# Moving hosted work to later slots in the expert stream of a fused two-layer transformer kernel

## What is computed

```python
for layer in range(DEPTH):
    y, y_x = token_mixer(modulate(x, sh1, sc1), modulate(ctx, xsh1, xsc1), w_in[layer], ...)
    x = layer_norm(alpha * x + g1 * y, ln1_g[layer], ln1_b[layer])
    f = peer(modulate(x, sh2, sc2), w_pq[layer], sub_keys[layer], u_tab[layer], v_tab[layer])
    x = layer_norm(alpha * x + g2 * f, ln2_g[layer], ln2_b[layer])
    # the context tokens go the same way, in layer 0 only

# peer, for a block of 128 tokens
q = (xb @ w_pq).reshape(128, 8, 2, 128)
s = einsum('thpd,hpnd->thpn', q, sub_keys)      # then top 16 of each half, top 16 of the 256 sums
u, v = u_tab[expert], v_tab[expert]             # 128 rows of each per token
a = gelu(einsum('td,thkd->thk', xb, u)) * softmax(top)
return einsum('thk,thkd->td', a, v)
```

## Time and profile before

| | us |
|---|---|
| median of three runs | 4543.57 |
| lowest, highest | 4536.91, 4545.58 |
| the profiled execution | 4533.96 |
| its span, first to last instruction | 4531.9 |

### The profile page before, as it was taken

The page is one execution under the profiler, slowest core; times in us unless marked ns, Lnnn a source line. Parts: engine busy times, 40 slices in busy tenths (PEclk is TensorE's granted clock), DMA queues, the critical chain, the costliest instruction groups (busy, mean ns, idle before and its releaser), DMA issues.

```text
span 4531.9 us, 47089 instructions
## 1 busy us (share of the span) xinstructions
PE 3090.0 (68%) x16196; PEld 1565.7 (35%) x16196; DVE 2892.1 (64%) x7342; ACT 823.3 (18%) x1929; POOL 2763.2 (61%) x2623
## 2 busy tenths in 40 slices
PE   7977787977678977645743778768698855443333
PEld 4443454444354343322310433445443422210000
DVE  4865677467676577556766663386756776766762
ACT  1321213122123131101110120221312310100100
POOL 1125666457667576657677665036666677777775
PEclk8989898998788998777865889989899976766556
DMA  8989999999999999999999999479999999999998
GB/s 326 331 296 403 398 408 383 367 360 406 404 406 393 409 388 396 407 408 404 393 397 366 397 392 408 170 260 410 395 390 401 371 404 408 403 382 394 399 405 332
DMA packets 494093, 1718.66 MB, mean 379 GB/s; under 512 B 54177, under 2 KB 74913, under 8 KB 493473
## 3 DMA queue, kind: packets, MB, share of 16 engines
q0 software_dynamic: 375552, 1367.51, 77.3%
q1 hardware_dynamic: 100640, 335.04, 19.2%
q10 hardware_dynamic: 17664, 13.11, 0.9%
HBM read 1700.25 MB, written 15.20 MB: 379 GB/s over the span
## 4 chain that ended last, share of the span: by engine, by line
PE 27%; POOL 26%; DMA 24%; issue 11%; DVE 9%; ACT 2%; SPq 0%; POOLq 0%; DVEq 0%; ACTq 0%
PE ps L983 26%; DMA vr<-in_v_tab,idxT 20%; POOL vr L956 14%; POOL ur L943 13%; DVE ur L2164 2%; PE ps L986 1%; DMA ur<-in_u_tab,idx 1%; DMA wring<-in_w_gb 1%; DMA wring<-in_w_mod 1%; DVE mx L2025 1%; DMA wring<-in_w_pq 1%; ACT arena L1490 0%; DVE rows L1836 0%; DVE vr L1836 0%; DVE mx L2023 0%
## 5 line engine op out<-in xcount | busy, mean ns | idle before, releaser
L2164 DVE CUSTOM_DVE_ANT_0 ur<-ur,hn 128x1024 f32<-128x1024 f32 x1280 | 1562.4, 1221 | 868.1 <-DMA ur<-in_u_tab,idx 864.2
L956 POOL DMA_INDIRECT vr<-in_v_tab,idxT x1256 | 1359.6, 1083 | 821.7 <-PE ps L983 485.2
L943 POOL DMA_INDIRECT ur<-in_u_tab,idx x1280 | 1351.9, 1056 | 753.0 <-issue 354.9
L983 PE MATMUL ps<-vr,spread 128*32 128x512 f32 x5024 | 889.0, 836 | 997.7 <-DMA vr<-in_v_tab,idxT 991.1
L983 PE MATMUL ps<-wring,arena 128*128 128x512 f32 (+1 forms) x2256 | 1025.4, 605 | 53.7 <-ACT arena L1490 15.2
L983 PEld LDWEIGHTS ps<-vr,spread 128*32 128x32 f32 x5024 | 180.7, 135 | 1490.7 <-issue 1488.6
L983 PEld LDWEIGHTS ps<-wring,arena 128*128 128x128 f32 x2256 | 422.3, 194 | 595.5 <-issue 529.1
L983 PE MATMUL ps<-hT,wring 128*128 128x128 f32 (+1 forms) x2048 | 315.9, 313 | 9.2 <-DMA wring<-in_w_pq 6.0
L983 PEld LDWEIGHTS ps<-hT,wring 128*128 128x128 f32 x2048 | 287.2, 199 | 76.3 <-issue 49.4
L986 PE MATMUL ps<-ident,arena 128*128 128x128 f32 x888 | 151.2, 306 | 119.6 <-ACT arena L1618 57.8
L983 PE MATMUL ps<-arena,wring 128*128 128x258 f32 (+1 forms) x960 | 223.5, 392 | 2.7 <-ACT arena L1577 2.2
(11 more groups left out here) (220 smaller groups left out, 2902.1 us busy)
## 6 DMA issues: line engine op xcount, KB each, us to landing
wring<-in_w_gb SPq DMA_DIRECT2D x224, 512.0 KB
wring<-in_w_pq SPq DMA_DIRECT2D x128, 512.0 KB
wring<-in_w_qkv SPq DMA_DIRECT2D x68, 512.0 KB
wring<-in_w_out SPq DMA_DIRECT2D x64, 512.0 KB
wring<-in_w_conv SPq DMA_DIRECT2D x60, 512.0 KB
wring<-in_w_mod SPq DMA_DIRECT2D x48, 512.0 KB
vr<-in_w_modt POOLq DMA_DIRECT2D x48, 512.0 KB, 7.8
ur<-in_u_tab,idx POOLq DMA_INDIRECT x1280
```

The costliest lines, as they stand in the source:

```text
L943: nc.gpsimd.indirect_dma_start(u, None, u_rows, bass.IndirectOffsetOnAxis(ap=idx[:, at:at + 1], axis=0)).then_inc(landed, 16)
L956: nc.gpsimd.indirect_dma_start(v, None, v_rows, bass.IndirectOffsetOnAxis(ap=idxT[:, pair % 3, i:i + 1], axis=0)).then_inc(landed, 16)
L983: return nc.tensor.matmul(o, lhsT, rhs, start=first, stop=last, skip_group_check=True)
L2164: v.tensor_tensor_reduce(u, u, hn[:], 1.0, 0.0, ALU.mult, ALU.add, dots[:, j % 2, k:k + 1]).then_inc(s["dots_done"], 1)
```

## The change

In tile 0 the loads of tile 1 stay at slot 0, and its near attention, first merge and ending stand at slots 12 to 64 instead of 0 to 62; the keys behind them at 64 to 74 instead of 62 to 74. In tile 6 the near keys stand at slot 11 instead of 0, the ending of tile 7 at 12 to 32 instead of 1 to 26, the reload at 32 instead of 26, and the remaining queries and the convolution at 42 to 69 instead of 33 to 68. No instruction and no transfer is added or removed.

```diff
@@ -292,8 +292,9 @@
         if n == 0:
-            put(near_part(1, team=1) + merge_first(1) + ending(1), 0, 62)
-            put(keys_job(1), 62, 74)
+            put([loads_of(1, team=1)], 0, 1)
+            put(near_part(1)[1:] + merge_first(1) + ending(1), 12, 64)
+            put(keys_job(1), 64, 74)
             put([[("turn", 1)], [("row", 0)], [("row", 1)], [("row", 2)]], 74, 78)
@@ -322,10 +323,10 @@
         elif n == 6:
-            put([[("nk", 0)]], 0, 1)
-            put(ending(7), 1, 26)
-            put(queries_job(4)[0:1], 26, 27)
-            put(queries_job(4)[1:] + conv_job(4), 33, 68)
+            put([[("nk", 0)]], 11, 12)
+            put(ending(7), 12, 32)
+            put(queries_job(4)[0:1], 32, 33)
+            put(queries_job(4)[1:] + conv_job(4), 42, 69)
             put([[("turn", 7)], [("row", 4)], [("row", 5)], [("row", 6)]], 74, 78)
```

## The result

The changed kernel takes **4573.4 us** (median, 4562.4 to 4590.4), beside 4543.1 us (4532.2 to 4549.7) for the kernel before on the same chip: ratio 1.0069, interval 1.0056 to 1.0083. It is slower, as forecast, but by 30 us instead of 12, and outside the range. The profiled execution has a span of 4584.2 us, 52.3 more than that of before.

What follows compares the result with a forecast made beforehand. The prediction took DMA, with a 410 GB/s ceiling, as the bound: unused DMA time adds 7.8 us (tile 6 to slot 32), 1 (its later slots) and 3.5 (tile 0), +12.3, giving 4556 us; own range 4547 to 4571.

Steps and rivals of the forecast that it cites:

- Bare slots: Slots 0 to 11 of tiles 0 and 6: 1.7 us each, set by DVE, 20.4 us with 2.4 unused.
- Attention: Tile 6's hosted attention: a chain of 38.8 us however few slots stand in it, 26.4 unused; tile 0's 26 us.
- Rival 1: Hosted chains in tiles 6 and 0 shrink with the slots in them: -5.4 us, 4538, not slower; chance 0.22.
- Merge of tile 6: Last merge with layer norm at slots 21.7 to 32: 38.4 us, 12.3 unused.
- Restart: Tile 6 after the ending: the reload waits for the ending's last write, now at slot 32; 2.6 us unused, as before.
- slot 40 is the next w_pq use, so nobody waits: Tile 6: w_pq chunks queued on SP behind the reload at slot 32 make no engine wait; no cost.
- rival 2: PE takes over from DMA in tile 6's slots 42 to 69 and tile 0's 41 to 64: 4566; chance 0.10.
- Tile 0: To slot 32, unused time rises from 12.9 to 16.4 us: +3.5, ends 0 and +6; later slots may leave 0 to 3 more.
- a longer wait costs nothing as long as transfers are queued: Tile 0 from slot 23: DVE's longer waits for merge chunks are free; far attention and end may leave 0 to 3 us.
- Nothing after slot 78 of either tile moves: Tiles 0 and 6 behind slot 78: stretches stay untouched, and any delay is simply carried to the end.
- rival 3: PE's lower clock level (1.2 GHz) holds for all of tile 6's attention: +5 us, 4561; chance 0.05.
- The sum: Whole kernel: 7.8 + 1 + 3.5 = +12.3 us, 4556 on the median, own range +3 to +27 us.

Runs made afterwards that it cites:

- e5: Kernel before with tile 6 hosting the ending of tile 7 at slots 1 to 16 instead of 1 to 26; ratio 1.0022.
- e10: Kernel before with only tile 6 changed: ending at slots 10 to 24, reload at 32, queries and convolution at 42 to 69; ratio 1.0033.
- e4: Kernel before with only tile 6's queries and convolution moved to slots 42 to 69, ending and reload as before; 4541.1 us, ratio 0.9993.
- e13: Tile 6 of the change alone, with the reload at slot 42 behind two w_pq chunks, queries at 43 to 69; 4550.5 us, ratio 1.0020.
- e11: Kernel before with only tile 0 changed: near attention stays at slots 0 to 13, merge and ending at 23 to 64, keys 64 to 74; ratio 0.9989.
- e8: Kernel before with only tile 0 changed: near attention, merge and ending at slots 12 to 70, keys at 70 to 74; ratio 1.0032.
- e1: Kernel before with only the change's tile 0 part (near attention, merge and ending at slots 12 to 64); 4551.1 us, ratio 1.0020.
- e18: The whole change with tile 6's reload at slot 42 behind two w_pq chunks, queries at 43 to 69; ratio 1.0023.
- e16: The kernel before, unchanged, run again for a trace on another chip; 4531.4 us.
- e12: Kernel before with tile 6's ending at slots 34 to 62, reload at 62, queries 63 to 86, near attention 90 to 127; ratio 1.0085.
- e9: Kernel before with tile 6's ending kept at slots 1 to 26, reload listed at 36, queries and convolution at 42 to 69; ratio 1.0002.
- e2: Kernel before with only the change's tile 6 part (ending at slots 12 to 32, reload 32, queries 42 to 69); 4558.6 us, ratio 1.0043.

## Why the prediction was right and wrong

**Bare slots: right.** Slots 0 to 12 of tile 6 took 20.0 us (forecast 20.4) with DVE busy 19.88 and 2.5 us unused (2.4). In tile 0 they took 19.0, with 3.1 unused (2.4).

**Attention: right.** From the first scores at 2995.73 to the merge it took 39.9 us (38.8) at 144 GB/s, unused 26.5 (26.4). In tile 0 the stretch from slot 12 to 24 took 26.9 (26), unused 10.7 (11.9). Rival 1 is refuted by this and by e5.

**Merge of tile 6: the term was mis-sized.** Forecast 38.4 us and 12.3 unused, measured 42.1 and 16.4. I had taken PE's part over from before, 25.8 us. But in before the query products of slots 24 and 25 stood behind it (at 3033.60), and the move brought the merge over those slots: 28.8 us with two products of 1.95 in it. e10 shows the same merge without them, 25.0. The tail was as before. Worth 4.1 us.

**Restart: the step "slot 40 is the next w_pq use, so nobody waits" failed.** The restart itself left 2.8 us (2.6). But the eight bare slots between the reload and slot 40 last only 16 us. Two w_pq chunks stood behind the reload on SP, and SP took 10.3 us to issue them while the first v gathers filled the engines. PE waits in order, so the v sums, the query products and POOL's v gathers wait with it. Slots 42 to 69 then carried what had been held up. I forecast 1 us there with ends 0 and 8; 4.6 us stand unused at slots 42 to 64. e4 shows that the dense queries by themselves cost nothing that can be told, and e13 that the order on SP is worth 6 to 9 us at slot 80. So rival 2 named the right stretch and the wrong cause: the rate did fall under 400 GB/s (396 and 388), but PE was not full, busy 37 of 44.4 and 47 of 55.8 us, and waited for the rest.

The Trainium skill ("DMA: Bandwidth & Descriptors", section "Rules for kernel authors") advises to issue a transfer early and to wait on it late. e13 agrees: with the two w_pq chunks issued 23 us ahead of the reload, PE's wait of 11.39 us for them is gone.

**Tile 0: forecast +3.5, ends 0 and 6, and 0 to 3 more; measured about +11.** This is the term that was furthest off. To slot 40 the sum holds: 17.7 us unused against my 16.4. What failed are two steps behind it. The first is "a longer wait costs nothing as long as transfers are queued", with the bound of 3 us for the rest: 4.5 us stand unused at slots 44 to 56. Neither density nor the shift of the near attention does this alone. e11 has the same density from slot 23 on without the shift and leaves nothing there; e8 has the shift with the work spread to slot 70 and leaves 0.1. By these single traces it takes both. The change's merge begins 15 to 16 us later than that of e11 or before, so its 32 chunks are squeezed: slots 24 to 40 took 70 us, 52 in e11. The slots behind then catch up, 2.3 us each from 44 to 52, with the DMA at 352 GB/s. That the rings of gathered rows are full by then, so that POOL has no place to fill, is my reading of it and not shown; the trace has one wait of POOL for PE in that stretch, 8.6 us before a v gather. The same tile 0 in e1 left 2.3 us there and in e18 0.9, so the size varies from run to run. The second step is "Nothing after slot 78 of either tile moves": at slots 80 to 96 the changed kernel leaves 2.7 us more than before and e1 2.9. e11 doesn't clear this up, and its cause stays open.

**The clock, rival 3: no part in tile 6, open in tile 0.** The attention of tile 6 ran at a granted 0.79, as before, the merge at 0.95 (0.97). Tile 0's near attention ran wholly at the lower level (1.2 GHz, granted 0.50), where before it had reached the upper one from about 300 us on. It still came near the forecast's 26 us, but this doesn't show that the clock costs nothing, for the work inside had changed too: its first scores had run ahead to 283.54, and the query products of slots 8 and 9 (3.78 and 2.05 us) no longer stood in it. Its value products follow each other by 6.5, 5.4 and 4.4 us at the lower level (304.78, 311.32, 316.71, 321.13); the last two before, at the upper level and with a query product between them, by 4.1 us (300.47, 304.54). So the clock may hold a few us here.

**The sum.** Tile 6: 8.8 forecast; with 4.1 from the merge and 3.6 more at slots 42 to 64 that is 16.5 of the 16.9 us of unused time. The tile is 19.7 us longer; the 2.8 between them stand unused at slots 64 to 128 (12.3 us, 9.7 before), where e16, the kernel before again, left 11.3, so I put them down to scatter. Tile 0: 11 instead of 3.5. Together 31 us, and the medians differ by 30.4. The recorded range ended at +27: its upper ends had nothing more for the merge and nothing behind slot 78. That the sum closes so well is in part luck, since each term is read from single traces that differ by 1 to 4 us among equal kernels. The profiled execution was 52 us longer than that of before; 18 of the other 21 are in tile 9 and no part of the change (below).

## What to carry to other kernels

A piece of work that is moved in a list shared by in-order engines takes a new place in every queue: list what now stands inside its chain (here two query products) and behind its waits (here two weight chunks on the issuing queue), and ask for each when it is needed in microseconds, not in slots. An issuing engine runs ahead of the list until a semaphore holds it, so a load that must wait for late results should stand behind the loads that needn't; here that one line was worth 4 to 9 of the 18 to 22 us that tile 6 had lost by slot 80. And a gain at one place (43 us to slot 64 in e12) is not yet one at the end: the displaced work has to find room for PE too.

## What the runs showed of the hardware

The last tile, where no kernel here changes anything, differs between executions. Before, the changed kernel, and e9 on another chip, from its first dot to its last:

```profile
4134.10:4464.20 330.10, 117.69 (x572) 27.29 (x572) 214.12 (x520) 21.37 (x37) 253.51 (x251) 0.57 1.01 400
```

```profile
4168.90:4516.80 347.90, 118.43 (x572) 27.32 (x572) 214.44 (x520) 21.37 (x37) 271.72 (x251) 0.60 0.99 379
```

```profile
4265.30:4633.00 367.70, 116.27 (x572) 26.93 (x572) 213.89 (x521) 21.40 (x37) 273.76 (x250) 0.60 0.96 359
```

The same 250 gathers pass at 400, 379 or 359 GB/s. Of other traces on the faster chips, e2 took 331.1 us and e16 328.9, e4 342.7. A difference of two single traces can thus hold 18 us that belong to neither kernel, which is why the tiles were compared one by one. On three of the chips the gathers alone ran at 356 to 372 GB/s in tiles 8 and 9, and the kernel before took 4680 to 4709 us, although in the bare slots, the attention and the first 80 slots of tile 0 those chips kept the same times.
